# Identity products that nobody reads, put into TensorE's order in front of its waits

## The reference, cut to what matters

```python
# first block
shift1, scale1, gate1, shift2, scale2, gate2 = split(silu(c) @ w_ada + b_ada, 6)
h = rms_norm(x, norm1_g) * (1 + scale1) + shift1
proj = h @ w_in                       # queries, keys, values, gates of two mixers
x = x + gate1 * (concat(gla_mixer(...), swa_mixer(...)) @ w_out)
h2 = rms_norm(x, norm2_g) * (1 + scale2) + shift2
x = x + gate2 * peer_mixer(h2)        # 128 of 16384 experts a row, by index: the gather
x = rms_norm(x, final_g)
# second block
proj = rms_norm(x, norm1_w) @ w_in_2
y = concat(diff_attention(...), stick_breaking_attention(...))
x = x + y @ w_out_2
u = rms_norm(x, norm2_w)
out = x + (silu(u @ w_gate) * (u @ w_up)) @ w_down
```

## Time and profile before

| what | value |
|---|---|
| median of 3 runs | 2427.0 us (2424.74 to 2427.84) |
| profiled execution | 2419.63 us, of which the span of the instructions is 2417.8 us |
| PE busy | 2037.8 us (84%), 7187 products |
| mean granted TensorE clock | 0.935 of 2.4 GHz |
| up to the gather, 0 to 400 us | PE busy 315.94 us, mean clock 0.87 |
| gather, 400 to 1966 us | PE busy 1337.60 us, mean clock 0.95 |
| after the gather, 1966 to 2417.8 us | PE busy 384.29 us, mean clock 0.93 |

### The profile page before, as it was taken

How to read it: one execution, slowest core, us unless ns; L and a number is a source line. 1 busy time by engine, 2 the same in 40 slices (tenths; PEclk the granted TensorE clock), 3 DMA queues, 4 the chain that set the end, 5 groups by cost and what they waited for, 6 DMA issues and landing times. The chain is left out here.

```text
span 2417.8 us, 22093 instructions
## 1 busy us (share of the span) xinstructions
PE 2037.8 (84%) x7187; PEld 1258.8 (52%) x7187; DVE 1507.7 (62%) x2989; ACT 994.5 (41%) x2304; POOL 911.8 (38%) x679
## 2 busy tenths in 40 slices
PE   7997758997998777777799888878999978787999
PEld 3775536544454322222465334445666646556887
DVE  5748456698895677755678875666777754442111
ACT  3216534433333222232444578344443335444443
POOL 3522002343443434343233434333343315205887
PEclk9997879998999999999899999899999989898999
DMA  7720055999999999999899999999999954103454
GB/s 269 265 103 1 1 183 218 381 420 377 399 416 374 420 421 422 421 420 421 340 391 376 421 374 343 385 374 378 421 421 421 421 202 139 52 1 104 174 192 157
DMA packets 111070, 726.58 MB, mean 301 GB/s; under 512 B 12519, under 2 KB 13546, under 8 KB 29802
## 3 DMA queue, kind: packets, MB, share of 16 engines
q0 software_dynamic: 74800, 540.59, 54.8%
q1 hardware_dynamic: 35520, 184.43, 20.4%
q10 hardware_dynamic: 634, 0.14, 0.0%
HBM read 716.45 MB, written 8.66 MB: 300 GB/s over the span
## 5 line engine op out<-in xcount | busy, mean ns | idle before, releaser
L1355 PE MATMUL ps<-uv_ring_a,expert_diag_a 128*128 128x512 f32 x1920 | 924.7, 628 | 201.6 <-ACT expert_diag_a L1334 183.1
L1123 POOL DMA_INDIRECT uv_ring_a<-in_peer_uv_dram,expert_idx x512 | 577.2, 1127 | 966.9 <-PE ps L1355 930.5
L1275 DVE CUSTOM_DVE_ANT_0 uv_ring_a<-uv_ring_a,x_rows 128x1024 f32<-128x1024 f32 x512 | 620.5, 1219 | 174.8 <-DMA uv_ring_a<-in_peer_uv_dram,expert_idx 173.9
L1355 PEld LDWEIGHTS ps<-uv_ring_a,expert_diag_a 128*128 128x128 f32 x1920 | 371.9, 200 | 672.6 <-issue 375.0
L1319 ACT ACTIVATE expert_gelu_a<-expert_dot_a 128x2 f32<-128x2 f32 x256 | 52.1, 204 | 788.1 <-DVE expert_dot_a L1275 788.0
L1445 POOL TENSOR_TENSOR w_low_b<-w_raw,w_high_b 128x1024 fp32r<-128x1024 f32 x96 | 229.0, 2392 | 243.4 <-ACT w_high_b L1437 192.9
L1445 DVE TENSOR_TENSOR w_low_a<-w_raw,w_high_a 128x1024 fp32r<-128x1024 f32 x142 | 173.6, 1223 | 186.7 <-ACT w_high_a L1437 186.1
L1437 ACT CAST w_high_a<-w_raw 128x1024 fp32r<-128x1024 f32 x146 | 151.0, 1038 | 92.6 <-PE ps L1458 76.7
L1334 ACT ACTIVATE expert_diag_a<-ident,expert_weight_a 128x128 f32<-128x128 f32 x480 | 168.8, 395 | 1.5 <-PE ps L1355 0.9
L1437 ACT CAST w_high_b<-w_raw 128x1024 fp32r<-128x1024 f32 x98 | 102.5, 1051 | 115.8 <-PE ps L1458 75.1
L1325 ACT ACTIVATE expert_weight_a<-expert_gelu_a,expert_gate 128x1 f32<-128x1 f32 x512 | 122.8, 286 | 8.9
(11 more groups left out here) (464 smaller groups left out, 3239.5 us busy)
## 6 DMA issues: line engine op xcount, KB each, us to landing
w_raw<-in_w_gu_dram SPq DMA_DIRECT2D x44, 1024.0 KB, 5.3
w_raw<-in_w_in_dram SPq DMA_DIRECT2D x24, 1024.0 KB, 5.5
w_raw<-in_w_down_dram SPq DMA_DIRECT2D x22, 1024.0 KB, 7.5
w_raw<-in_w_out_dram SPq DMA_DIRECT2D x16, 1024.0 KB, 6.9
w_raw<-in_w_peer_q_dram SPq DMA_DIRECT2D x16, 1024.0 KB, 9.1
in_raw<-in_w_in_dram SPq DMA_DIRECT2D x20, 512.0 KB, 6.1
uv_ring_a<-in_peer_uv_dram,expert_idx POOLq DMA_INDIRECT x512, 12.5
swab<-in_w_ada_dram SPq DMA_DIRECT2D x13, 512.0 KB, 5.6
```

Source lines behind the costliest of these rows:

```text
L1123: pool.indirect_dma_start(out=self.ring[:, n % self.RING, :], out_offset=None, in_=K.uv, in_offset=bass.IndirectOffsetOnAxis(ap=K.idx[self ...
L1275: dve.tensor_tensor_reduce(u, u, self.h[b][:, :], 1.0, 0.0, ALU.mult, ALU.add, self.a[:, s:s + 1]).then_inc(self.s_dot, 1)
L1355: ins = nc.tensor.matmul(self.bank(half), self.diag[q % self.DIAGS][:, :], self.ring[:, n % self.RING, D + 512 * half:D + 512 * half + 512 ...
```

## The change: spare products in front of waits

A new function `keep_busy(K, b, n)` issues n plain products of the identity with itself (128 by 128 by 128, float32) into bank b. Nothing reads the result, no semaphore is touched, and each bank is written by real work, from its first column on, before anything reads it. In `Swa` and `Diff` the wait for the bank's last copy is moved in front of the wait for the data, and the spare products stand between the two. `Turn`, `Diff` and `Stick` take a new argument `idle` with numbers of products; its default is none, so in `stage_first` only the first tail's `Turn` gets any (40).

```diff
+def keep_busy(K, b, n):
+
+    for _ in range(n):
+        K.nc.tensor.matmul(K.ps[b][:, 0:P], K.ident[:, :], K.ident[:, :], start=True, stop=True)
...
@@ stage_front
             last.then_inc(s_m1, 1)
+            keep_busy(K, 2, 24)
             for n in range(VG):
...
                         mm(nc, K.ps[1 + n][:, :], K.ones[:, :], sums2[:, 3 * D + 512 * n:3 * D + 512 * n + 512]).then_inc(s_gr, 1)
+            keep_busy(K, 7, 10)
@@ Swa.pe
         def turn(i):
-            pe.wait_ge(self.s_n, i + 1)
             if i >= 1:
                 pe.wait_ge(self.s_te, i)
+            keep_busy(K, 6, 3 if i else 34)
+            pe.wait_ge(self.s_n, i + 1)
...
         self.norm.sums(pe)
+        keep_busy(K, 6, 26)
@@ Turn.pe
         yield self.at
+        keep_busy(self.K, self.idle[0], self.idle[1])
         for sem, value in ready:
             pe.wait_ge(sem, value)
...
             ins.then_inc(self.s_t, 1)
+        keep_busy(self.K, self.idle[0], self.idle[2])
@@ Diff.pe
-            pe.wait_ge(self.s_n, i + 1)
             if i >= 2:
                 pe.wait_ge(self.s_te, i - 1)
+            keep_busy(self.K, self.banks["t"][i % 2], self.idle[i == n - 1])
+            pe.wait_ge(self.s_n, i + 1)
@@ Stick.pe
         yield self.at[0]
+        keep_busy(self.K, self.banks["o"][0], self.idle[0])
         for sem, value in self.ready:
             pe.wait_ge(sem, value)
...
             yield self.at[t] + 0.3 * self.us
+            if t == 1:
+                keep_busy(self.K, self.banks["o"][0], self.idle[1])
@@ Tail
-        self.turn = Turn(K, tag + "h", x, split, [K.ps[j][:, :] for j in range(4)], [1.0] * KD, self.at_n[1])
+        self.turn = Turn(K, tag + "h", x, split, [K.ps[j][:, :] for j in range(4)], [1.0] * KD, self.at_n[1], (7, 0 if before else 40, 0))
@@ stage_first
             last.then_inc(s_kt, 1)
+            keep_busy(K, 7, 22)
...
                                     t2.pe(pe, stick.done()), o2.pe(pe), t3.pe(pe, [n2.done]), ffn.pe(pe)))
+            keep_busy(K, ffn.up[-1], 36)
@@ stage_half: the new last argument of each
+            t1 = Turn(..., at[0], (6, 0, 9))
+            diff = Diff(..., (3, 14))
+            stick = Stick(..., (12, 8))
+        t2 = Turn(..., at[0], (6, 14, 7))
+        t3 = Turn(..., at[1], (6, 20, 6))
```

More of the change, by code:

```diff
@@ L1462, with __init__ @@
 class Turn:
-    def __init__(self, K, name, src, dst, banks, gains, at):
+    def __init__(self, K, name, src, dst, banks, gains, at, idle=(0, 0, 0)):
         self.K, self.src, (self.hi, self.lo), self.banks, self.gains, self.at = K, src, dst, banks, gains, at
+        self.idle = idle
         self.nb = len(src)
@@ L1798, with __init__ @@
 class Diff:
-    def __init__(self, K, plan, half, ready, bias, banks, turn_ready=(), values_ready=()):
+    def __init__(self, K, plan, half, ready, bias, banks, turn_ready=(), values_ready=(), idle=(0, 0)):
+        self.idle = idle
         self.K, self.half, self.ready, self.bias, self.banks = K, half, ready, bias, banks
@@ L1985, with __init__ @@
     PAIRS = ((0, 2), (1, 3), (4, 6), (5, 7))
-    def __init__(self, K, plan, half, ready, banks):
-        self.K, self.half, self.ready, self.banks = K, half, ready, banks
+    def __init__(self, K, plan, half, ready, banks, idle=(0, 0)):
+        self.K, self.half, self.ready, self.banks, self.idle = K, half, ready, banks, idle
         self.nb, self.b0, self.b1 = half.nb, half.b0, half.b0 + half.nb
@@ L2806, in stage_half @@
             t1 = Turn(K, "in2_rows", [un[:, b, :] for b in range(nb)], split, four,
-                      [K.vecT[:, V_N12 + k:V_N12 + k + 1] for k in range(KD)], at[0])
+                      [K.vecT[:, V_N12 + k:V_N12 + k + 1] for k in range(KD)], at[0], (6, 0, 9))
             p2 = In2Early(K, W, plan, half, t1, [un[:, i, :].rearrange("p (a b) -> p a b", a=2) for i in range(2)])
@@ L2810, in stage_half @@
             diff = Diff(K, plan, half, [(p2.s_te, 2 * nb)], (half.s_bm, 1),
-                        {"s": (0, 1), "t": (4, 5), "o": (6, 7)}, (), [(p2.s_val, nb)])
+                        {"s": (0, 1), "t": (4, 5), "o": (6, 7)}, (), [(p2.s_val, nb)], (3, 14))
         with ExitStack() as K.phase:
-            stick = Stick(K, plan, half, diff.done() + p2.done(), {"z": (0, 1), "r": (2, 3), "o": (4, 5)})
+            stick = Stick(K, plan, half, diff.done() + p2.done(), {"z": (0, 1), "r": (2, 3), "o": (4, 5)}, (12, 8))
         K.phase = ctx
@@ L2817, in stage_half @@
         t2 = Turn(K, "mix", [half.mix[:, b, :] for b in range(nb)], split, four,
-                  [K.diffw[:, 0:1]] * 4 + [K.vecT[:, V_SBN:V_SBN + 1]] * 4, at[0])
+                  [K.diffw[:, 0:1]] * 4 + [K.vecT[:, V_SBN:V_SBN + 1]] * 4, at[0], (6, 14, 7))
         o2 = Out2(K, W, plan, half, t2, (4, 5, 0, 1))
@@ L2822, in stage_half @@
         t3 = Turn(K, "ffn_rows", [un[:, b, :] for b in range(nb)], split, four,
-                  [K.vecT[:, V_N22 + k:V_N22 + k + 1] for k in range(KD)], at[1])
+                  [K.vecT[:, V_N22 + k:V_N22 + k + 1] for k in range(KD)], at[1], (6, 20, 6))
         ffn = Ffn(K, W, plan, half, t3, (4, 5, 6, 7), (0, 1, 2, 3))
```

## The result

| | before | after |
|---|---|---|
| median of the timed executions | 2426.72 us (7 runs, 2420.8 to 2427.84) | 2412.92 us (7 runs, 2405.23 to 2416.68) |
| ratio to before | 1 | 0.9945, 95% interval 0.9929 to 0.9961 |
| profiled execution | 2419.63 us, span 2417.8 | 2405.23 us, span 2403.5 |
| mean granted TensorE clock | 0.935 | 0.960 |

The change makes the kernel 13.8 us faster. The forecast was 2419.6 us; 2412.92 lies inside the range, near its low end.

A forecast was written before the change was run, and what follows sets the result against it. Transfers bound the gather; outside it TensorE ran 165.8 us at half clock, which spare products in waits should shorten. Ten sites sum to -7.4 us, from the median 2427.0 to 2419.6 us; range 2411.5 to 2428.5.

The forecast's parts named there:

- The price of a spare product: Duration assumed for one spare product, taken from transposes of the same shape: 0.13 us at full clock, 0.23 at half.
- Site 1: Front, 24 spare products in the wait of 6.18 us: they fit and may speed the 9 slow products behind; -0.9 us.
- Sites 2 and 3: Mixers: 34 spare products in the first wait, -1.7 us; three at each of 15 later turns, +1.0 us.
- the mixers hold their clock: Rival, chance 0.10: threes at the mixers' turns win back some 7 us of 13.9 more; about 2412.5 us.
- Sites 4 and 5: First tail, 22 in 6.23 us: -1.1 us; 10, 26 and 36 at block and stage ends, 40 in 10.79 us: 0.
- site 10: Waits of `t2` (14 and 7 spare products) and `t3` (20 and 6): less slow work, -3.0 us for both.
- site 6: `t1`, 9 spare products in the wait of 3.21 us: faster products behind it, -1.5 us.
- Site 9: `stick`, 12 spare products in 3.35 us and 8 in 2.33 us: both fit, slow stretch behind gets shorter; -1.5 us.
- Sites 7 and 8: `diff`: seven times 3 in front of waits, -0.5 us; 14 at the eighth turn without a wait, +1.8 us.
- the clock falls again: Rival, chance 0.25: spare products end early in waits beginning at full clock, slow work returns; 2424.9 us, no change.
- half clock well under 165.8 us: Sign of being right: stretches at half clock outside the gather sum to well under the 165.8 us of before.
- the gather begins 2 to 4 us earlier: Sign of being right: gains ahead of the gather arrive as a start 2 to 4 us earlier.

The follow-up runs named there:

- e7_before_again: The kernel before, without an edit, profiled for a second trace; 2421.63 us in the single execution.
- e1_behind_only: The change with spare products only behind the gather, its swapped waits kept; 2419.73 us, ratio to before 0.9959.
- e2_ahead_only: The change with spare products only ahead of the gather (none in t1, diff, stick, t2, t3); 2418.38 us, ratio to before 0.9963.
- e12_change_again: The change without an edit, run once more on the chip of the later kernels; 2410.6 us, ratio to before 0.9941.
- e4_transposes: The change with every spare product a transpose of the identity, same places and counts; 2424.22 us, ratio to before 0.9974.

## Why the prediction was right in sign and half in size

The starts of TensorE's instructions on the timelines cut the run into eight parts. "Without" is before and `e7_before_again`, and as third trace `e1_behind_only` ahead of the gather and in it, `e2_ahead_only` behind it, since these parts have no spare products there; "with" is the change's two traces. All in us:

| part (sites of the prediction) | forecast | without | with | mean |
|---|---|---|---|---|
| start to first scores of the mixers (1) | -0.9 | 182.1, 184.1, 182.8 | 183.3, 183.8 | +0.6 |
| first scores to norm (2, 3) | -0.7 | 119.1, 125.9, 130.0 | 120.3, 117.3 | -6.2 |
| norm to the gather's first product (4, 5) | -1.1 | 123.5, 124.1, 123.8 | 121.9, 122.3 | -1.7 |
| gather | 0 | 1534.2, 1529.9, 1532.4 | 1529.0, 1534.0 | -0.7 |
| gather's last product to first turn of `diff` (6) | -1.5 | 70.7, 69.4, 69.4 | 67.5, 68.1 | -2.0 |
| turns of `diff` to `stick` (7, 8) | +1.3 | 72.2, 70.7, 70.8 | 73.7, 72.5 | +1.8 |
| `stick` to `t2` (9) | -1.5 | 81.0, 81.0, 81.0 | 77.6, 80.1 | -2.1 |
| `t2` to TensorE's last product (10) | -3.0 | 230.7, 230.6, 230.4 | 226.0, 225.8 | -4.7 |
| sum | -7.4 | | | -15.0 |

The medians differ by 13.8 us in the first comparison and by 14.8 in the last. With two or three traces a mean of a part is good to a microsecond or so, in the mixers to several. The spans of the two traces of before and the two of the change differ by 13.0 us; most of what is left of the 15.0 comes in with the mixers of `e1_behind_only`.

- **The price of a spare product failed, by a factor of two.** The prediction took it from the transposes of the earlier trace rows. But a plain float32 product of 128 by 128 by 128 is two records and 0.22 us at full clock (14 of them at 2168.52 us: 3.34 us with the tail of the last), a transpose one record and 0.11. This could have been read in the trace of before: 16 steps of scores with two products each are there 64 records of `kTd` and `rqT`, while 64 transposes of `swa_p` are 64. Outside the trace there was a figure too: the Trainium skill (FP8 and Floating Point Precision, TensorE Precision Notes) gives a true float32 product four passes through the array. Four times 128 columns at 2.4 GHz are 0.21 us, an estimate from that page, and the trace agrees with its 0.22.
- **Site 1** brought nothing (+0.6, where a part without spare products scatters by 2). The products behind the wait are fast, as forecast, but the 24 run 0.4 us (48.8 for 48.4 us) to 2.2 us (50.6, `e12_change_again`) past it, and then TensorE waits for DVE. Nor was it the wait that brought the clock down here. In before the clock fell at 42.1 us, before the wait of 6.18 us had begun, while TensorE was at work without a pause on 16 one-column products (32 records) that start at 38.4 us. In `e12_change_again` it fell at 40.6 us, the rest of these records took 0.21 us each in place of 0.11, and the spare products began 1.5 us later than in the first trace (43.3 for 41.8).
- **Sites 2 and 3** are the term that was mis-sized most: -6.2 us in place of -0.7. The rival "the mixers hold their clock", given 0.10, was what happened (0.86 and 0.91 in place of 0.66 to 0.77); it forecast 2412.5 us. That the measured 2412.92 lies so near it is in part luck, since its other terms are those of the sum. The reason that I held against it, a DVE nearly as busy as TensorE, is true of the first slow stretch and was misread for the five that the rival speaks of: there DVE is busy for 15.07 us and TensorE for 27.76. In `e7_before_again` and `e1_behind_only` there is more such work: TensorE 22.86 us and DVE 14.19 in a slow stretch of 27.3 us from 255.9 us on, and TensorE 39.96 and DVE 7.75 in one of 44.4 us from 271.5 us on. And the profiled execution of before was 7.4 us quicker than the median. I carried that as a constant. It should have been a question: in which stage was it lucky? By the second and third trace it was this one. (The second trace of before, 2421.63 us, was quicker than its median, 2427.11, as well.)
- **Sites 4 and 5**: -1.1 forecast, -1.7 measured. The 22 overran (328.84 us minus the start of `turn_keys`' products at 319.08 is 9.8 us; 9.4 before), but the tail behind is shorter. The 40, at twice the price, filled 8.9 of 10.79 us and made the first tail's 16 transposes fast in the first trace (1.97 us), not in `e12_change_again` (3.55). I had put that at 0. The 16 of `t1` behind the 36 stayed slow, as forecast (3.01 and 3.65 us).
- **Sites 6, 9 and 10** paid more than forecast. For site 10 the reason is that double the price filled the waits that I expected to be left half empty: 14 ahead of `t2` left 1.41 us of 4.58, 20 ahead of `t3` 1.28 of 5.75, and `e4_transposes`, at half the price, won 2.5 us there in place of 4.7 (3.0 were forecast). For site 6 the price is not the reason: `e4_transposes` was as quick there (68.1 us). Site 9 takes one of two lengths: 77.6 us in five traces with its spare products, 80.1 in three others, against 81.0 without. The difference is between the first `tri` product and the values: 15.7 us in the first trace of the change, 18.1 in the second, 19.0 before.
- **Sites 7 and 8**: +1.3 forecast, +1.8 measured. The bare 14 last 3.1 us, not 1.8 (this sign of being right, 1.5 to 1.8 us of spare products ahead of the eighth turn, failed), and the threes are too few in front of the long wait ([4.10] left at the seventh turn).
- The rival **"the clock falls again"** was built on holes of 2.8 and 3.2 us that did not come to be. `e4_transposes`, where they did, shows part of it: behind the gather 453.5 us, against 449.0 to 450.8 with the change.
- Of what was to show that the prediction was right: half clock well under 165.8 us was right (71.5), products 0.23 us apart behind the waits was right within the first two, "the gather begins 2 to 4 us earlier" was wrong against the profiled execution (425.5 for 424.7) and an understatement against the other two (434.0 and 436.6).

So the mechanism was right and the sum was too small, by two errors that point the same way: a price too low and a stage seen at its best. The second is the larger, 5.5 of the 7.6 us between the forecast sum of -7.4 and the -15.0 of the table.

## What to carry to other kernels

Price an instruction by the records it becomes, and count them against the program before taking a neighbour's duration. Where the profiled execution lies off the median by as much as the effect that is forecast, take a second trace and find the stage that scatters: a change that steadies a stage pays at the median what it does not pay in a lucky trace. Put filler where the wait is, sized to end just before it does. Past a wait it costs its full length, and short of it the clock may fall. Look also at what TensorE did when the clock fell: in the front and at 155 us it was at work, on one-column products.

## What the runs showed of the hardware

- A plain float32 product of 128 by 128 by 128 is two records, 0.22 us at full clock; a transpose of the same shape one record, 0.11 us. 24, 34 and 22 spare products during which the clock rose from half to full (at 46.3, 193.1 and 326.2 us) took 7.0, 10.3 and 7.1 us, 0.29 to 0.32 us each.
- Transposes of the identity hold and raise the granted clock nearly as products of the same duration do: ratio 0.9921 (0.9889 to 0.9952) and 0.9912 (0.9894 to 0.9929), 0.97 and 0.98 behind the gather.
- Products of one column, one behind the other with no idle time between them, do not hold the clock: it fell within the run of 32 of them (64 records) from 154 us on in all 14 traces. They follow the clock themselves, 0.11 us from record to record at full and 0.21 at half.
- The same instructions on one core, with the same data, take 119.1 to 130.0 us in the mixers from one execution to the next, with the clock at 0.66 to 0.77 and no other engine's work changed. A stage with short bursts and waits has no fixed speed. Behind the gather the same comparison gives 455.8 to 459.9 us over four traces.
